# Low parts of five weight blocks from GpSimd to VectorE, and small input loads put in another order

## Time and profile before

| | us |
|---|---|
| median of 3 runs | 763.28 (758.41 to 764.7) |
| the profiled execution | 763.2, span 761.6 |
| TensorE busy | 698.4 (92%) |
| VectorE busy | 245.6 (32%) |
| ScalarE busy | 191.8 (25%) |
| GpSimd busy | 44.7 (6%) |
| DMA | 243.72 MB, mean 320 GB/s |

### The profile page before, as it was taken

One profiled execution on the slowest core, in us unless ns is written; L12 is line 12 of the kernel. 1 busy time (PEld: TensorE's weight loads), 2 busy tenths in 40 slices (PEclk: granted clock), 3 DMA queues, 4 the chain that ended last, 5 costly groups with the idle time before them and its releaser, 6 DMA issues.

```text
span 761.6 us, 9953 instructions
## 1 busy us (share of the span) xinstructions
PE 698.4 (92%) x4027; PEld 412.6 (54%) x4027; DVE 245.6 (32%) x472; ACT 191.8 (25%) x297; POOL 44.7 (6%) x17
## 2 busy tenths in 40 slices
PE   4899999989978596999999999899998898998994
PEld 4899877767757475444434444343443343453431
DVE  6453446655766716212111111111111111111112
ACT  5442446577544126010000001000000000000003
POOL 0000002030320404000000000000000000000000
PEclk9999999989999799899999999999999999999997
DMA  9698531353444858699999999999999999999992
GB/s 305 214 308 293 167 111 56 111 166 111 136 133 135 353 220 335 279 382 428 427 429 427 424 426 426 426 425 427 426 426 427 426 428 426 427 427 427 418 382 81
DMA packets 44150, 243.72 MB, mean 320 GB/s; under 512 B 10000, under 2 KB 12232, under 8 KB 31560
## 3 DMA queue, kind: packets, MB, share of 16 engines
q1 hardware_dynamic: 43672, 241.45, 79.9%
q0 software_dynamic: 432, 1.59, 0.6%
HBM read 241.96 MB, written 1.07 MB: 319 GB/s over the span
## 4 chain that ended last, share of the span: by engine, by line
PE 69%; DMA 17%; DVE 4%; issue 3%; SPq 3%; ACT 2%; POOL 1%; POOLq 0%; ACTq 0%; DVEq 0%
PE bank L1497 24%; DMA unit<-in_w 16%; PE bank L1531 9%; PE bank L1217 8%; PE bank L1218 7%; PE bank L1219 7%; PE bank L1475 4%; PE bank L1543 2%; PE bank L1544 2%; DMA sinks<-in_swa_sinks 1%; POOL br_low L509 1%; PE bank L1295 1%; PE bank L1507 1%; SPq L368 1%; SPq L371 1%
## 5 line engine op out<-in xcount | busy, mean ns | idle before, releaser
L1497 PE MATMUL bank<-unit,xT 128*64 128x512 f32 x1024 | 231.5, 605 | 12.8 <-DMA unit<-in_w 9.2
L1497 PEld LDWEIGHTS bank<-unit,xT 128*64 128x64 f32 x1024 | 75.8, 139 | 153.2 <-issue 148.9
L1531 PE MATMUL bank<-unit,hidT 128*64 128x512 f32 x512 | 113.6, 595 | 0.7 <-issue 0.7
L1217 PE MATMUL bank<-high,hT_hi 128*128 128x512 f32 (+2 forms) x224 | 84.3, 376 | 4.9 <-DVE low L301 3.9
L1218 PE MATMUL bank<-low,hT_hi 128*128 128x512 f32 (+2 forms) x224 | 82.3, 367 | 0.0
L1219 PE MATMUL bank<-high,hT_lo 128*128 128x512 f32 (+2 forms) x224 | 82.2, 367 | 0.0
L1531 PEld LDWEIGHTS bank<-unit,hidT 128*64 128x64 f32 x512 | 35.6, 137 | 65.9 <-issue 64.4
L301 DVE TENSOR_TENSOR low<-unit,high 128x2048 fp32r<-128x2048 f32 (+1 forms) x32 | 66.1, 2085 | 11.4 <-ACT high L296 11.4
L296 ACT ACTIVATE high<-unit 128x2048 fp32r<-128x2048 f32 (+1 forms) x34 | 58.9, 1754 | 15.1 <-PE bank L1219 10.1
L1122 DVE TENSOR_TENSOR y_lo<-bank,y_hi 128x512 fp32r<-128x512 f32 x32 | 22.1, 692 | 104.0 <-ACT y_hi L711 104.0
L1475 PEld LDWEIGHTS bank<-pick,hk 128*128 128x128 bf16 x768 | 46.7, 101 | 13.8 <-issue 13.6
(11 more groups left out here) (214 smaller groups left out, 704.6 us busy)
## 6 DMA issues: line engine op xcount, KB each, us to landing
unit<-in_w SPq DMA_DIRECT2D x88, 2048.0 KB, 29.3
unit<-in_w_gate SPq DMA_DIRECT2D x8, 2048.0 KB, 10.0
unit<-in_w SPq DMA_DIRECT2D x12, 1024.0 KB, 27.9
unit<-in_w_in SPq DMA_DIRECT2D x3, 2048.0 KB, 14.8
unit<-in_w_in SPq DMA_DIRECT2D x4, 1024.0 KB, 9.1
unit<-in_w_br SPq DMA_DIRECT2D x4, 1024.0 KB, 5.3
unit<-in_w_o SPq DMA_DIRECT2D x2, 2048.0 KB, 10.2
unit<-in_w SPq DMA_DIRECT2D x8, 512.0 KB, 17.1
```

Source lines behind the costliest of these rows:

```text
L1217: mm(dst, a_hi, b_hi, start=first, stop=False)
L1497: last = mm(bank[4 + w][g * CAP:(g + 1) * CAP, :], xT[:, k, g * CAP:(g + 1) * CAP], rhs, start=(k == 0), stop=(k == KD - 1))
L1531: last = mm(bank[6 + n][g * CAP:(g + 1) * CAP, :], hidT[:, c, g * CAP:(g + 1) * CAP], rhs[:, c, n * BANK:(n + 1) * BANK], start=(c == 0), ...
```

## The change

GpSimd's four br_low and its two halves of w_o's second block are made by VectorE instead, with the same operation on the same tiles: br_low after VectorE's low part in st 3, 7, 11 and 13, w_o's halves after `merged_low(1)`. SP's router loads become a function of their own, issued behind weight block 8 (u = 7), and the constants' second part moves behind the nine "small" inputs, which so follow block 2 (u = 1) directly.

```diff
             sp.dma_start(gmix[:], ...).then_inc(s["cst"], 16)
 
-            def small_loads():
-                sp.dma_start(cst[:, C_GE:], a["constants"][:, C_GE:]).then_inc(s["tri"], 16)
+            def router_loads():
                 sp.dma_start(gffn[:], ...).then_inc(s["wr"], 16)
                 sp.dma_start(wr[:, :, 0:NG], ...).then_inc(s["wr"], 16)
                 sp.dma_start(wr[:, :, NG:], ...).then_inc(s["wr"], 16)
                 sp.dma_start(rbias[:, 0:NG], ...).then_inc(s["wr"], 16)
                 sp.dma_start(rbias[:, NG:], ...).then_inc(s["wr"], 16)
+
+            def small_loads():
                 sp.dma_start(relb[:], a["rel_bias"]).then_inc(s["small"], 16)
...
                 sp.dma_start(sinks[:], ...).then_inc(s["small"], 16)
+                sp.dma_start(cst[:, C_GE:], a["constants"][:, C_GE:]).then_inc(s["tri"], 16)
...
                 if u == 1:
                     small_loads()
+                if u == 7:
+                    router_loads()
...
             pool.dma_start(bias[:], ...).then_inc(s["biasT"], 16)
-            for b in range(4):
-
-                u, w, hi, lo = branch_parts(b)
-                pool.wait_ge(s["brh"], b + 1)
-                nc.gpsimd.tensor_tensor(lo, w, hi.bitcast(F32), ALU.subtract).then_inc(s["brl"], 1)
-
-            pool.wait_ge(s["low"], split_count(14, KD - 1))
-            for half in range(2):
-                low_part(pool, nc.gpsimd, 15, half)
...
                 elif st < 15:
                     low_part(dve, nc.vector, 7 + st // 2, st % 2)
+                if st in (3, 7, 11, 13):
+                    u, w, hi, lo = branch_parts(st // 4)
+                    dve.wait_ge(s["brh"], st // 4 + 1)
+                    nc.vector.tensor_tensor(lo, w, hi.bitcast(F32), ALU.subtract).then_inc(s["brl"], 1)
...
             merged_low(1)
+            for half in range(2):
+                low_part(dve, nc.vector, 15, half)
```

## The result

The changed kernel takes 740.99 us (median of 4 runs, 739.81 to 742.7) against 763.13 (4 runs) for the kernel before: ratio 0.9699, interval 0.9653 to 0.9745, 3% faster. The profiled execution took 742.13 us with a span of 740.6, so the two profiled executions are 21.1 us apart; the forecast was 18.6 for them, and 744.6 in all.

A forecast was written before the change was run, and what follows sets the result against it. The expert stage was taken as a weight stream at its ceiling, so TensorE's waits and low-clock stretches up to about 300 us count: 2.6 - 1.9 + 0.3 + 1.3 + 5.6 + 10.7 = 18.6 us, 763.2 to 744.6, range 740 to 751.

The forecast's parts named there:

- rival 3: Expert weight stream does not follow the whole shift, only 7.9 us of it: 755.3 us; chance 5%.
- rival 1: TensorE's low clock also stays away after the second branch's norm wait, worth 3.1 us: 741.5 us; chance 10%.
- (c): Second branch, st 7: norm wait of 2.52 us goes, 2.25 given back in the next wait; gain 0.3 us.
- (a): Start: small inputs issued some 10 us sooner, TensorE's 2.63 us wait goes; gain 2.6 us, bounds 0 and 2.6.
- (b): First branch, st 3: VectorE gets 2.25 us more work ahead of its next scores; loss 1.9 us.
- (d): Third branch, st 11: L855 sheds 3.52 us, low part adds 2.25; TensorE's 2.83 us wait becomes 1.5; gain 1.3.
- (e): Fourth branch, st 13: all 3.92 us of wait go, plus 1.7 of low clock; gain 5.6 us.
- (f): Merge: 7.7 of TensorE's 8.47 us wait go, plus 3.0 of slow clock; gain 10.7 us.
- (g): w_o's two low parts behind merged_low(1): 4.5 us on VectorE, covered by a TensorE product that doesn't need them; cost 0.
- Router loads: Five issues after weight block 8, at their old 10.3 us, just fit the 10.9 us before block 9; cost 0.
- Rival 2: New exposed wait in VectorE's order, for w_o's low halves (4.5) or the last scores (2.3): 751.4 us; chance 6%.
- Rival 4: Something other than GpSimd holds VectorE; long instructions stay and six low parts add 13.5 us: 774.1 us; chance 4%.

The follow-up runs named there:

- experiment 1: Only the new order of SP's small loads, low parts left on GpSimd, against the kernel before: 760.0 us, ratio 0.9914 (0.9879 to 0.9948).
- experiment 2: Only the six low parts moved to VectorE, loads in the old order, against the kernel before: 748.16 us, ratio 0.9759.
- experiment 3: Only w_o's two low halves moved to VectorE, br_low on GpSimd, loads in the old order, against the kernel before: 754.77 us, ratio 0.9826.
- experiment 4: Changed kernel plus one unused GpSimd subtraction of 128x2048 that reads x: 748.53 us, ratio 0.9763 to the kernel before.
- experiment 6: The changed kernel timed again, nothing altered: 742.39 us, ratio 0.9701 to the kernel before.
- experiment 5: Changed kernel plus one unused GpSimd memset of 128x2048 floats, which reads nothing: 743.55 us, ratio 0.9712 to the kernel before.

## Why the prediction was right

- **What bounds the kernel.** Right. The gathering came 20.1 us earlier and the end 21.0; rival 3, a stream that doesn't follow, falls.
- **The whole.** The time came out 3.6 us under the forecast, at 741.0, next to the 741.5 of rival 1. That rival's cause gave 0.2 us, as (c) shows; most of the difference is the start.
- **(a) Start**, the one term whose size was off: 2.6 forecast, 3.7 between the two profiles, and 6.6 (4 to 9) by the times of experiment 1. The step took one execution's wait as the most that could be gained. In the changed kernel's trace TensorE was ready at 26.46 and not at 27.55, because its matmuls became faster sooner. The same matmuls of block 0, before and after:

```profile
18.42 0.41 PE L1218 MATMUL bank<-hT_lo,high 128*128 128x256 f32 x1
...
18.84 0.28 PE L1217 MATMUL bank<-hT_hi,high 128*128 128x256 f32 x1
```

```profile
16.24 0.41 PE L1218 MATMUL bank<-hT_hi,high 128*128 128x256 f32 x1
...
16.63 0.28 PE L1220 MATMUL bank<-hT_hi,low 128*128 128x256 f32 x1
```

Until 18.6 us before, and until 16.5 after, they take 0.41 us and start 0.21 us apart, as matmuls of this size do at 0.50 in the window of experiment 2; then 0.28 and 0.12. The profile has no clock below 1.00 on record this early, so that this is the low clock is read from the durations. The moment varies between executions: in the traces of experiments 2 and 3 the matmuls of block 0 are fast from the second on, at 13.2 us, in all others from between 16.6 and 19.1. In the old order a TensorE that is ready early only waits longer (4.30 and 4.72 us in experiments 2 and 3) and in both these traces runs on at the low clock. The table product started at 30.18, 28.91 and 29.32 us in the three traces of the old order and between 26.36 and 27.67 in the eight of the new one, 2.5 us earlier in the mean. With 3.4 us of low clock behind it in two of the three, an estimate is 4.8 us, within the interval of experiment 1. No trace in the new order was ready as early as 24.6 us, so what the new order would give there isn't shown.
- **(b) First branch**: a loss of 1.9 forecast, 1.7 measured (a wait of 1.88 instead of 0.16).
- **(c) Second branch**: a gain of 0.3 forecast and measured at the value product. The 2.52 us of the wait for the norm came back there, almost whole (0.45 became 3.11). Rival 1 asked for a full clock behind it. The low stretch was there: 0.75 over the old window instead of 0.51, but it only started later, at the branch product instead of at the turning of the heads. From the value product to the end of the next gate half TensorE took 6.83 us instead of 7.07, so it was worth 0.2.
- **(d) Third branch**: 1.3 forecast. TensorE was 2.5 us ahead when it came to this product (ready at 206.14 against 208.68) and 4.0 when it started; the wait is 1.40 instead of 2.83, so 1.4 measured.
- **(e) Fourth branch**: 5.6 forecast. TensorE was 4.0 us ahead up to the wait for the gate's low part and 9.7 at the value product behind it (224.92 against 234.62): 5.7 measured, the wait and the low clock.
- **(f) Merge**: 10.7 forecast, 7.7 + 2.7 = 10.4 measured.
- **(g) Halves of w_o**: 0 forecast and measured; no wait for them.
- **Router loads**: forecast to fit in 10.9 us at 10.3; they took 10.7, and no TensorE wait appeared.
- **Rival 2** falls: TensorE has no wait for the last scores or for w_o's halves.
- **Rival 4**, VectorE held by something else, falls by experiments 3 and 4.

The sum of the terms as measured is 3.7 - 1.7 + 0.5 + 1.4 + 5.7 + 10.4 = 20.0, as TensorE's lead of 20.1 us at the gathering has it, and the profiled pair is 21.1 apart. These are terms of one pair of executions. How long the clock stays low behind a wait is partly chance: the changed kernel's second trace (experiment 6), with the same waits, has a mean clock of 0.57 from 165 to 173 us, the first 0.79, and TensorE takes 0.8 us longer from the value product to the third branch product.

What stays open is why one execution reaches the full clock earlier than another at the start, and where the last 0.9 us behind the gathering come from.

## What to carry to other kernels

When an instruction on one engine takes several times as long as its equals, look at what another engine runs at that moment and where both end; the price of work on GpSimd was not its own 4.5 us but what it held on VectorE. Before costing moved work, find the idle gaps of the engine that takes it, and put it there: the same six low parts gave 3.0% where they were first put and 3.7% in VectorE's gaps. A wait that is removed is worth more than its length where the low clock stands behind it, and less where the next thing in the queue is late too.

## What the runs showed of the hardware

- GpSimd's reading subtraction held VectorE's two-input instruction for all that it had left to run; its memset of the same size did not (experiments 4 and 5). The addition that started in the same instant as GpSimd's subtraction ran its 0.69 us.
- The hold goes the other way as well. In the kernel before, GpSimd's four br_low took 5.52, 6.38, 6.72 and 4.55 us. VectorE low parts of the same size that were running when they started had 1.1, 1.9 and 2.3 us left beside the first three, and none ran beside the fourth, so each took about 4.5 us from there on (three of the four in the earlier trace rows). The one beside the third, at 202.07 us:

```profile
202.06 2.29 DVE L301 TENSOR_TENSOR low<-unit,high 128x2048 fp32r<-128x2048 f32 x1
```

- Not every VectorE instruction is held. While that br_low ran on, two of L832, `prob<-bank,bias` with one input in PSUM, took 0.29 us (at 204.38) and 0.42 us (at 204.60), and 0.28 and 0.42 us in the changed kernel, where GpSimd is idle (at 223.93 and 224.14).
- A wait of about 1.9 us can, but need not, be followed by the low clock. Behind the first branch product, in the memset kernel and in the changed kernel:

```profile
124.60:128.00 3.40, 3.24 (x8) 2.59 (x9) 2.22 (x9) 1.09 (x1) 0.00 (x0) 0.50 0.02 5
```

```profile
123.90:127.30 3.40, 3.40 (x15) 2.77 (x16) 3.29 (x8) 1.52 (x2) 0.00 (x0) 1.00 0.02 5
```

The waits were 1.89 and 1.88 us; the granted clock was 0.50 in one and 1.00 in the other. Up to there the two kernels run the same instructions. From this product to the value product of st 8, TensorE took 42.6 us in one and 41.2 in the other, so the same code with the same waits can differ by about 1.5 us.
